# One fused transformer pair on one core: eleven small moves in the order of each engine's work

## What is computed

```
# first block (adaLN, six modulations), context of 256 tokens
mod = silu(c) @ w_mod + b_mod
h  = modulate(x, norm1_g, sh1, sc1);  px = h @ w_in          # and the same for ctx
GLA, 4 heads, both directions, chunks of 64:
    S_t = diag(alpha_t) S_{t-1} + k_t^T v_t ;  o_t = q_t S_t
differential attention, 4 heads, 512 queries x 768 keys:
    p = softmax(q k / 8) for two components;  o = (p0 - lam * p1) @ v
x = x + gt1 * (concat(rmsnorm(o_gla) * silu(r), rmsnorm(o_diff)) @ w_out)
x = x + gt2 * swiglu(modulate(x, norm2_g, sh2, sc2))

# second block (nine modulations)
x = x + 0.5 * gt1 * swiglu(modulate(rmsnorm(x)))
proj = modulate(rmsnorm(x)) @ w_in_2      # q_a k_a v_a, q_idx k_idx w_idx, c_q c_kv k_rope, gates
index: score = sum_h w_idx[h] * relu(q_idx[h] . k_idx); top 128 keys of each query
DSA : softmax over the selected keys with a T5 bias, 8 heads, one shared k_a, v_a
MLA : q from w_uq(rmsnorm(c_q)), k,v from w_uk, w_uv(rmsnorm(c_kv)), rotary part of 32, 8 heads
x = x + gt2 * ((sigmoid(g_a) * (o_a @ w_o_a) + sigmoid(g_b) * (o_b @ w_o_b)) @ w_out)
x = x + 0.5 * gt3 * swiglu(modulate(rmsnorm(x)));   out = rmsnorm(x)
```

## Time and profile before

| what | value |
|---|---|
| median of 3 runs | 1982.98 us |
| profiled execution: its time, its span | 1986.12 us, 1984.3 us |
| mean granted TensorE clock | 0.993 of full |
| TensorE busy | 1937.7 us (98%) |
| VectorE, ScalarE, GpSimd busy | 919.3, 756.5, 702.1 us |
| chain that ended last | TensorE 90%, VectorE 5%, DMA 2%, ScalarE 2% |

### The profile page before, as it was taken

How to read it: one execution, slowest core, us unless ns; L and a number is a source line. 1 busy time by engine, 2 the same in 40 slices (tenths; PEclk the granted TensorE clock), 3 DMA queues, 4 the chain that set the end, 5 groups by cost and what they waited for, 6 DMA issues and landing times.

```text
span 1984.3 us, 28048 instructions
## 1 busy us (share of the span) xinstructions
PE 1937.7 (98%) x11158; PEld 1559.7 (79%) x11162; DVE 919.3 (46%) x1465; ACT 756.5 (38%) x1299; POOL 702.1 (35%) x295
## 2 busy tenths in 40 slices
PE   8999999999999999999999999999999999999998
PEld 5778867788888888888888887657766898888886
DVE  2757568554444410544443354666875342322102
ACT  4553336443222213422222145664356343222212
POOL 1423301124444445244444433321411434444442
PEclk9989999999999999999999999999999999999999
DMA  7851100215444544244445532211311333333331
GB/s 320 305 213 44 44 12 22 86 43 169 138 148 138 181 146 136 87 138 150 142 163 185 177 91 84 75 43 33 96 44 33 89 93 95 95 95 95 95 95 64
DMA packets 61291, 223.38 MB, mean 113 GB/s; under 512 B 6928, under 2 KB 9232, under 8 KB 59536
## 3 DMA queue, kind: packets, MB, share of 16 engines
q1 hardware_dynamic: 60624, 219.70, 34.2%
q10 hardware_dynamic: 576, 2.43, 0.4%
HBM read 220.00 MB, written 2.10 MB: 112 GB/s over the span
## 4 chain that ended last, share of the span: by engine, by line
PE 90%; DVE 5%; DMA 2%; ACT 2%; issue 1%; SPq 0%; DVEq 0%; ACTq 0%
PE ps L450 79%; DMA mod_w<-mod_w 1%; DMA early_raw<-early 1%; PE ps L1116 1%; DVE neg_max L1249 1%; PE ps L2566 1%; PE ps L2737 1%; PE ps L2758 1%; PE ps L1753 1%; PE ps L995 0%; PE ps L2588 0%; PE ps L2728 0%; PE ps L1097 0%; PE ps L1017 0%; PE ps L2746 0%
## 5 line engine op out<-in xcount | busy, mean ns | idle before, releaser
L2132 POOL TENSOR_TENSOR w_lo<-raw,w_hi 128x1024 fp32r<-128x1024 f32 x262 | 634.8, 2423 | 1240.0 <-ACT w_hi L463 640.9
L450 PE MATMUL ps<-hh,w_hi 128*128 128x512 f32 (+1 forms) x1496 | 585.6, 391 | 7.4 <-DVE ki_lo L2279 2.1
L450 PE MATMUL ps<-hh,w_lo 128*128 128x512 f32 (+1 forms) x1496 | 577.1, 386 | 0.0
L450 PE MATMUL ps<-hl,w_hi 128*128 128x512 f32 (+1 forms) x1496 | 577.1, 386 | 0.0
L450 PEld LDWEIGHTS ps<-hh,w_hi 128*128 128x128 f32 x1496 | 282.1, 189 | 74.1 <-issue 13.4
L450 PEld LDWEIGHTS ps<-hh,w_lo 128*128 128x128 f32 x1496 | 282.1, 189 | 57.5
L450 PEld LDWEIGHTS ps<-hl,w_hi 128*128 128x128 f32 x1496 | 282.4, 189 | 54.0
L2105 ACT ACTIVATE w_hi<-raw 128x1024 fp32r<-128x1024 f32 x126 | 133.7, 1061 | 469.9 <-PE ps L450 469.9
L516 DVE SCALAR_TENSOR_TENSOR mod_raw<-mod_raw,cond_ada 128x1024 f32<-128x1024 f32 x72 | 110.5, 1536 | 259.3 <-DMA mod_raw<-late 259.3
L450 PE MATMUL ps<-act_hi,w_hi 128*128 (+1 forms) x480 | 189.6, 395 | 0.0
L450 PE MATMUL ps<-act_hi,w_lo 128*128 (+1 forms) x480 | 189.6, 395 | 0.0
(11 more groups left out here) (495 smaller groups left out, 2645.8 us busy)
## 6 DMA issues: line engine op xcount, KB each, us to landing
raw<-stream SPq DMA_DIRECT2D x284, 512.0 KB, 3.6
mod_raw<-late SPq DMA_DIRECT2D x72, 512.0 KB, 4.6
early_raw<-early SPq DMA_DIRECT2D x32, 512.0 KB, 6.0
mod_w<-mod_w SPq DMA_DIRECT2D x8, 1024.0 KB, 20.3
xT<-xT SPq DMA_DIRECT2D x2, 1024.0 KB, 6.1
xT<-xT ACTq DMA_DIRECT2D x2, 1024.0 KB, 6.4
out<-fin SPq DMA_DIRECT2D x16, 128.0 KB, 1.9
cT<-cT SPq DMA_DIRECT2D x1, 1024.0 KB, 21.6
```

Source lines behind the costliest of these rows:

```text
L450: mm = pe.matmul(out, w, r, start=first and i == 0, stop=last and i == 2, skip_group_check=open_group)
L2132: pool.tensor_tensor(lo[:, :], raw[n % RING][:, :], hi[:, :].bitcast(F32), ALU.subtract)\
```

## The change

Nothing is computed that was not computed before; instructions change their place, three products change their bank, seven waits become finer, and one table load moves. Cut to the core:

```diff
 # diff_scalar
-            if u in (1, 2):
-                key_decay(act, u - 1)
-            if u == 4:
-                meanwhile()
+            if u in DECAY_AT:
+                key_decay(act, *DECAY_AT[u])
+            if u in (10, 11):
+                meanwhile(u - 10)          # split_slots(firsts["mix1_diff"] + 0, then + 1)
+    DECAY_PARTS = (0, 1, 2)                # edges, tiles 0 to 2, tiles 3 to 5
+    DECAY_AT = {4 + part + 3 * i: (i, (part,)) for i in range(2) for part in DECAY_PARTS}
 # gla_tensor: the 20 state products of direction 0 between the second and third spread
+        for h in range(HEADS):
+            if h == 2:
+                state_products(0)
...
-                b = (6, 7, 0)[j // 2]
+                b = ((6, 7, 0) if i else (7, 0, 3))[j // 2]
 # gla_vector
-        for h in range(2, HEADS):
-            gated_output(h)
-        for pair in range(2):
-            if pair:
-                output_roots(1)
-            for h in (2 * pair, 2 * pair + 1):
-                output_scaled(h)
-            for h in (2 * pair, 2 * pair + 1):
-                output_low(h)
+        gated_output(2)
+        output_scaled(0)
+        gated_output(3)
+        output_low(0)
+        output_scaled(1)
+        output_low(1)
+        output_roots(1)
+        for h in (2, 3):
+            output_scaled(h)
+        for h in (2, 3):
+            output_low(h)
 # half_sums, second half of the last norm only
+            if one_by_one:
+                pe.wait_ge(*norm(name, "sq", i + 1))
 # proj2_vector
-        rope2_vector(dve, 0.25)
         b = full(dve, ("ki", 0))
         dve.wait_ge(S("ki_hi"), 1)
         dve.tensor_tensor(ki_lo ...)
+        rope2_vector(dve, 0.25)
         for h in range(4):
             lower_parts(dve, "qi", h, qi_views, 1.0)
-            if h == 0:
+            if h == 1:
                 rope2_vector(dve, 0.0)
 # lora_scalar, mla_scalar, mla_tensor
     def lora_scalar(act):
+        exps_ahead(act)
...
-        split_slots(act, second["g_gated_b"] + 1)
+            if p in (4, 8):                # in mla_scalar, behind outputs(p - 1)
+                split_slots(act, second["g_gated_b"] + p // 8)
-        read(pe, ("vb", 3))
+            if p == 0:                     # in mix_values(0)
+                read(pe, ("vb", 3))
 # dsa_tensor, dsa_scalar
-        logits_tensor(pe, [(0, k) for k in range(KD)])
+        logits_tensor(pe, [(0, k) for k in range(LOGITS_FIRST)])      # 4
...
         scores(0)
         scores(1)
+        logits_tensor(pe, [(0, k) for k in range(LOGITS_FIRST, KD)])
...
-        logits(0)
         exps(0)
         signs(2)
+        logits(0)
 # gated_vector_b
+        rounds = (3, 2, 3, 2, 3, 2, 1, 0)
-            for _ in range(ROUNDS // KD):
+            for _ in range(rounds[m]):
                 topk_round(dve)
-            if m == KD - 1:
+            if m == KD - 2:
                 topk_end(dve)
```

More of the change, by code:

```diff
@@ L1208, in diff_scalar, with key_decay, key_edges @@
             act.dma_start(xT[:, 4 * i:4 * i + 4, :], A["xT"][:, 4 * i:4 * i + 4, :]).then_inc(S("x_again"), 16)
-    def key_decay(act, i):
+    DECAY_PARTS = (0, 1, 2)
+    DECAY_AT = {4 + part + 3 * i: (i, (part,)) for i in range(2) for part in DECAY_PARTS}
+    def key_decay(act, i, parts=DECAY_PARTS):
+        d, pc = directions[i]
+        sources = ((cumc[:, d, pc * NCTX:(pc + 1) * NCTX], 0, NTC), (cumx[:, d, pc * N:(pc + 1) * N], NTC, NT))
+        if 0 in parts:
+            key_edges(act, i, sources)
+        tiles = [(src, t0, t) for src, t0, count in sources for t in range(count)]
+        for part in (1, 2):
+            if part in parts:
+                for src, t0, t in tiles[3 * part - 3:3 * part]:
+                    ins = act.activation(sq[i % 2][:, (t0 + t) * P:(t0 + t + 1) * P], src[:, t * P:(t + 1) * P], ACT.Exp,
+                                         bias=to_edge[:, d, pc, t0 + t:t0 + t + 1], scale=-GATE_SCALE)
+        if 2 in parts:
+            ins.then_inc(S("edge_decay"), 1)
+    def key_edges(act, i, sources):
         d, pc = directions[i]
@@ L1225, in key_decay @@
         settle(act, "edge_step")
[L1226 to L1230, removed]
     def decayed_keys(dve, i):
@@ L1486, in gla_tensor, with state_products @@
         keys_turned(0)
[L1487 to L1497, removed]
+        def state_products(i):
+            d, pc = directions[i]
             read(pe, ("kA", i))
@@ L1508, in gla_tensor @@
                 mm.then_inc(bank_full(b), 1)
+        for h in range(HEADS):
+            if h == 2:
+                state_products(0)
+            b = (6, 5)[h % 2]
+            claim(pe, b, ("no", h), norm("no", "t1", h + 1))
+            pe.wait_ge(*norm("no", "rs", 1))
+            for t in range(NT):
+                mm = pe.transpose(ps[:, b, t * P:(t + 1) * P], rs["no"][:, h * NT + t:h * NT + t + 1].broadcast_to([P, P]), ident)
+            mm.then_inc(bank_full(b), 1)
+        for i in range(len(directions)):
+            if i:
+                keys_turned(i)
+            mixed_values_chunk(pe, 2 * i)
+            if i:
+                state_products(i)
             mixed_values_chunk(pe, 2 * i + 1)
@@ L1749, in half_sums @@
         claim(pe, ba, name + "_ss")
-        pe.wait_ge(*norm(name, "sq", KD if h == 0 else len(HALVED[key])))
+        one_by_one = key == "ffn3" and h == 1
+        if not one_by_one:
+            pe.wait_ge(*norm(name, "sq", KD if h == 0 else len(HALVED[key])))
         for i, k in enumerate(chunk_order(key)):
             q = i % 4
+            if one_by_one:
+                pe.wait_ge(*norm(name, "sq", i + 1))
             mm = pe.matmul(ps[32 * q:32 * q + 32, ba, 0:HALF_T], c("one").broadcast_to([P, 32]), sq_all[:, k, part(h)], start=(i < 4), stop=(i >= 4))
@@ L2694, in build @@
     AHEAD_A = KD - 1
+    LOGITS_FIRST = 4
     logit_steps = [(1, 3), (1, 3), (1, 2), (2, 3), (2, 3), (2, 2), (3, 4), (3, 4), (4, 3), (4, 3), (4, 2), (5, 4), (5, 4), (6, 3), (6, 3), (6, 2)]
@@ L3000, in gated_vector_b @@
     def gated_vector_b(dve):
+        rounds = (3, 2, 3, 2, 3, 2, 1, 0)
+        assert sum(rounds) == ROUNDS
         for m in range(KD):
-            for _ in range(ROUNDS // KD):
+            for _ in range(rounds[m]):
                 topk_round(dve)
-            if m == KD - 1:
+            if m == KD - 2:
                 topk_end(dve)
@@ L3137, in _ @@
         projections_scalar(act)
-        diff_scalar(act, lambda: split_slots(act, firsts["mix1_diff"] + 1))
+        diff_scalar(act, lambda more: split_slots(act, firsts["mix1_diff"] + more))
         gla_scalar(act)
```

1 line of the change is left out of this document (removed).

## The result

The changed kernel takes 1991.13 us (median of 6 runs, 1990.67 to 1994.39), the kernel before 1982.76 us beside it (6 runs, 1980.88 to 1985.06). The ratio is 1.0039, with a 95% interval from 1.0028 to 1.005: slower by more than the 0.2% of the prediction. The likeliest case was 1984.5 us, and the range ended at 1990.5, so the median lies 0.6 us above it. The profiled execution took 1991.09 us, its span is 1989.3 us.

A forecast was written before the change was run, and what follows sets the result against it. TensorE, busy 98% of the span, was taken to bound the kernel, so edits count only through its idle time or half clock. Terms -3.5+3.6-1.0+3.6+1.4+2.4-4.2-0.8 = +1.5 on 1982.98 gave 1984.5 us; range 1974 to 1990.5.

The forecast's parts named there:

- The claims of banks 3 and 0: TensorE waits for VectorE's release: mixed chunk 2 in GLA, `cq` 0 behind the index key; +3.6 us each with half clock.
- MLA's start: Start of MLA: table load, two splits and the wait for the last value copy go; -1.6 us.
- the gated outputs: Gated outputs reordered: the first low half comes one multiplication earlier, so a waiting product starts sooner; -1.0 us.
- DSA: Top-k and DSA: four of eight logit steps go between scores 1 and 2, so scores 3 start earlier; -4.2 us.
- the last norm: Last norm: seven of eight products over the squares run before the last square is there; -0.8 us.
- Rival 1: GLA, index key, MLA: the new waits don't come, bank claims find their banks free; -14.0 us, 1969; chance 0.12.
- Rival 2: MLA and the sine: GpSimd comes too late to hold VectorE; sum -3.9 us, 1979.1; chance 0.23.
- the splits in differential attention: Attention: GpSimd's low half begins behind the wide subtraction, ends ahead of the next narrow one; may cost some tenths.
- The gain of the decays: Differential attention: decays in pieces fit ScalarE's idle time, so units shorten; stage -3.5 us, bounds -3.9 and -2.3.
- MLA's splits: MLA: two weight splits behind `outputs(3)` and `outputs(7)` let GpSimd hold VectorE's scaling of `mp`; 2.0 us each, +4.0.
- The table load: Head of the up-projections: a load and small `Exp` ahead of the first `qb` copy delay the rotation; +1.4 us.
- rival 3: The waits bring half clock, mainly at MLA's two held scalings, also in DSA and index key; +6.7 us, 1989.7; chance 0.20.

The follow-up runs named there:

- the repaired kernel: The changed kernel with five placements moved (attention splits, sine, table load, MLA's splits, state products back where the kernel before has them; chunk 2 in bank 3): 1969.31 us.
- the five repairs: The changed kernel with one placement moved each: attention splits 1990.88, chunk 2's bank 1991.02, sine 1988.47, table load 1993.12, MLA's splits 1986.56 us.
- the four put-backs: The repaired kernel with one placement of the change put back each: MLA's splits 1977.33, sine 1976.34, state products with bank 3 1973.53, attention splits 1972.17 us.

## Why the prediction was right or wrong

**Right: the waits and their releasers.** The claims of banks 3 and 0 (3.29 us against 3.2, 5.62 against 5.8), the rotation (1.55 against 1.4), the held scaling in MLA (1.91 against 2.2), MLA's start, the gated outputs, DSA and the last norm came as the timelines had them, each within 0.3 us of its forecast in waits or terms. Rival 1 is refuted as a forecast: both claims wait. With the waits taken out all comes to 1969, its figure, though not by all of its terms: it had -1.2 for the state products and +1.4 for the load, and the repaired kernel has 0 and +0.5. Rival 2 (GpSimd misses VectorE) did not happen at either place.

**Wrong: the splits in differential attention, by 4.5 us.** The step was that GpSimd's low half "begins behind the wide subtraction of probabilities and ends just ahead of the next narrow one, so it may cost some tenths". That nearly holds for the first split, which ScalarE issued at 314.73: it cost 0.4 us. The second was issued with more lead and its low half began 0.05 us ahead of the subtraction, so one unit did not stand for the next. The gain of the decays was forecast right (3.4 us by unit 6), but the wait of 2.13 us at the second split and 1.7 us of half clock behind it took back more than that. Moved behind the units the splits leave the stage at -3.07, put back alone they cost 3.7 us. The Trainium skill ("SBUF — State Buffer", section "Who interferes with whom") has the lock between the two for whole instructions, and the 3.11 us of unit 11, the 2.70 in MLA and the 2.45 in the sine agree; the prediction applied it in MLA and not here.

**Mis-sized: the clock behind the new waits.** The term of MLA's splits was 4.0, idle time alone; it measured 6.8, and 8.8 in the term and in the median when nothing else was wrong. Of these, 3.4 and 5.1 us are half clock in the profiled executions. The table load was 1.4 and measured 3.1: 1.55 of wait and 1.5 at half clock, and 1.5 in all in an execution in which the clock did not fall there. The Trainium skill ("ScalarE: Activation LUTs", "What ACT_TABLE_LOAD costs") would have given 2.8 by a drain behind the load; the trace has 0.02 us there, so the near match is by another cause. The claim of bank 3 was 3.6 with half clock; the profiled execution had 2.1 without, four others 5.0 to 6.0 with it. So rival 3, with its place in MLA and its price of 1989.7, came closest: both scalings were held for the whole low half and the clock fell. Its DSA part failed: that stage kept its 4.1 us. That its total came so near is partly luck: it was too high in GLA, MLA and DSA by 3.4 us together, and too low in attention, load and index key by 6.6. Its MLA term is also mis-added: 2.2 + 1.6 twice, less 1.6, is +6.0 and not +5.6, which makes 1990.1.

**The sum.** +1.5 was forecast, +8.4 came in the median. In the profiled terms the misses are 4.5 (differential attention), 2.8 (MLA), 1.7 (load), 1.0 (index key) and -1.5 (GLA): 8.5 of the 8.7 between +1.5 and +10.2. The -5.2 us at the head of the trace is no part of it. It is half clock that the kernel before had there and the changed one had not, and the profiled executions of the twelve experiments, with that stretch unchanged too, have between -5.3 and -0.1 there.

## What to carry to other kernels

Where GpSimd holds SBUF for 2.4 us, place each of its instructions by which one VectorE instruction it meets, at each place anew: 0.05 us decided over 2 us here, and beside PSUM work it was free. When a bank is passed to another user, ask which instruction of which engine frees it, and what stands ahead of that one. And judge a repair of one stage by its term in the trace and by its put-back in a repaired kernel, not by one median alone: the five repairs returned some 8 us of medians one by one and 22 together, while the four put-backs cost what their stages' terms say.

## What the runs showed of the hardware

- The hold between VectorE and GpSimd works both ways: GpSimd's low half took 2.95 us behind a VectorE instruction under way, and VectorE's 3.11 instead of 1.02 behind GpSimd's. GpSimd also got in between two scalings of VectorE queued back to back.
- The same waits in the same order brought more half clock in some executions than in others (GLA's term +2.1 or +5 to +6, MLA's splits +6.8 to +10.4; the first 270 us, the same in all kernels, held 0 to 5.1 us of it). The kernel before has 14 to 15 us of its 1983 by span times (1 - clock) on the mean, of which 2.4 us in its profiled execution fell in the last 10 us, where TensorE is mostly idle.
- A table load of 1.28 us had no drain behind it: the next instruction of ScalarE came 0.01 to 0.02 us behind it at 28 of the 29 loads of the kernel before, and at the other ScalarE waited 2.9 us for TensorE.
